# Splitting 768-column products into 384 and 384 columns, one half per PSUM bank, in place of 512 and 256

## The reference, cut to what matters

```python
for i in range(DEPTH):                     # DEPTH = 2
    h_lat = modulate(rmsnorm(x, g_mix_pre[i]), ...)
    h_ctx = modulate(rmsnorm(xc, g_mix_pre[i]), ...)
    if last:
        s_f, s_b = context_states(h_ctx, ...)      # k, v and decay columns of w_in alone
    else:
        y_ctx, s_f, s_b = token_mixer(h_ctx, *mix_w, s0, s0)
        xc = ffn_sublayer(xc + ..., ...)
    y_lat, _, _ = token_mixer(h_lat, *mix_w, s_f, s_b)   # p = h @ w_in; ... ; y @ w_out
    x = ffn_sublayer(x + ..., ...)                       # (silu(a) * u) @ w_ffn_out, a | u = h @ w_ffn_in
```

## Time and profile before

| what | value |
|---|---|
| time, median of 3 runs | 1666.36 us (1664.7 to 1668.96) |
| span of the profiled execution, first to last instruction | 1662.6 us |
| mean granted TensorE clock | 0.990 |
| PE busy | 1589.5 us, 96% |
| PEld busy | 1344.1 us |
| DVE, ACT, POOL busy | 729.6, 568.3, 587.4 us |

### The profile page before, as it was taken

How to read it: one execution, slowest core, us unless ns; L and a number is a source line. 1 busy time by engine, 2 the same in 40 slices (tenths; PEclk the granted TensorE clock), 3 DMA queues, 4 the chain that set the end, 5 groups by cost and what they waited for, 6 DMA issues and landing times.

```text
span 1662.6 us, 23266 instructions
## 1 busy us (share of the span) xinstructions
PE 1589.5 (96%) x9328; PEld 1344.1 (81%) x9328; DVE 729.6 (44%) x1206; ACT 568.3 (34%) x918; POOL 587.4 (35%) x309
## 2 busy tenths in 40 slices
PE   5999999999899999999999989999989999999997
PEld 2778877877689989998999767787877888888887
DVE  2500325845656515662366673045754321221137
ACT  4533213524634313441244254432523422232231
POOL 1522211334424524553255223222132444444441
PEclk9999999999999999999999999999999999999999
DMA  9444332154312212222122343531071222222221
GB/s 372 167 166 149 127 114 71 39 206 180 152 39 77 89 38 77 77 72 75 56 77 69 134 152 104 176 112 53 27 279 52 89 92 97 93 96 100 90 87 66
DMA packets 49166, 182.37 MB, mean 110 GB/s; under 512 B 5106, under 2 KB 10098, under 8 KB 42164
## 3 DMA queue, kind: packets, MB, share of 16 engines
q1 hardware_dynamic: 42930, 167.28, 28.5%
q10 hardware_dynamic: 6146, 13.83, 2.4%
HBM read 169.55 MB, written 11.53 MB: 109 GB/s over the span
## 4 chain that ended last, share of the span: by engine, by line
PE 85%; DVE 5%; ACT 3%; DMA 3%; POOL 1%; issue 1%; SPq 1%; DVEq 0%; ACTq 0%; POOLq 0%
PE A L981 58%; PE A L1227 8%; PE N L1227 4%; PE G L1227 4%; DMA raw<-stream 2%; PE N L1001 1%; PE G L1282 1%; DMA raw<-modw 1%; PE A L1123 1%; PE G L1089 1%; SPq L848 1%; PE G L1001 1%; PE N L1073 1%; PE G L1130 1%; PE A L1161 1%
## 5 line engine op out<-in xcount | busy, mean ns | idle before, releaser
L919 POOL TENSOR_TENSOR w_lo<-raw,w_hi 128x1024 fp32r<-128x1024 f32 (+2 forms) x163 | 379.9, 2333 | 709.9 <-ACT w_hi L1309 672.7
L981 PE MATMUL A<-h_hi,w_hi 128*128 128x512 f32 (+1 forms) x1264 | 415.8, 360 | 22.8 <-POOL h_lo L964 11.7
L981 PE MATMUL A<-h_hi,w_lo 128*128 128x512 f32 (+1 forms) x1264 | 406.7, 353 | 0.0
L981 PE MATMUL A<-h_lo,w_hi 128*128 128x512 f32 (+1 forms) x1264 | 405.9, 352 | 0.0
L1309 ACT ACTIVATE w_hi<-raw 128x1024 fp32r<-128x1024 f32 (+2 forms) x163 | 167.0, 1028 | 389.5 <-PE A L981 342.1
L981 PEld LDWEIGHTS A<-h_hi,w_hi 128*128 128x128 f32 x1264 | 223.2, 190 | 80.8 <-POOL h_lo L964 18.5
L981 PEld LDWEIGHTS A<-h_hi,w_lo 128*128 128x128 f32 x1264 | 223.9, 190 | 32.7
L981 PEld LDWEIGHTS A<-h_lo,w_hi 128*128 128x128 f32 x1264 | 223.4, 190 | 31.4 <-issue 0.5
L981 PE MATMUL A<-g_hi,w_hi 128*128 128x512 f32 (+1 forms) x480 | 147.8, 351 | 3.8 <-DVE g_lo L1790 2.0
L981 PE MATMUL A<-g_lo,w_hi 128*128 128x512 f32 (+1 forms) x480 | 146.8, 349 | 0.0
L981 PE MATMUL A<-g_hi,w_lo 128*128 128x512 f32 (+1 forms) x480 | 146.7, 349 | 0.0
(11 more groups left out here) (308 smaller groups left out, 2570.2 us busy)
## 6 DMA issues: line engine op xcount, KB each, us to landing
raw<-stream SPq DMA_DIRECT2D x150, 512.0 KB, 3.3
mraw<-modw SPq DMA_DIRECT2D x38, 1024.0 KB, 4.8
raw<-pairs SPq DMA_DIRECT2D x18, 512.0 KB, 4.7
raw<-modw SPq DMA_DIRECT2D x6, 1024.0 KB, 14.7
x<-x_keep ACTq DMA_DIRECT2D x4, 1536.0 KB, 14.3
raw<-stream SPq DMA_DIRECT2D x16, 384.0 KB, 3.0
mraw<-pairs SPq DMA_DIRECT2D x9, 512.0 KB, 3.4
x_keep<-x SPq DMA_DIRECT2D x4, 768.0 KB, 22.4
```

The source lines that it names most:

```text
L919: pool.tensor_tensor(lo, like_chunk(n, raw[:, n % RAW, 0:WIDTH[n]]), hi.bitcast(F32), ALU.subtract).then_inc(lo_done, 1)
L981: m = pe.matmul(dst[:, t0:t1], a, b[:, k, t0:t1], start=(first and p == 0), stop=(last and p == 2))
```

## The change

`in_banks` takes the place of `segments` in the products of 768 tokens: tokens 0 to 383 go to columns 0 to 383 of the accumulator's first bank, tokens 384 to 767 to columns 0 to 383 of its second bank (512 to 895 of the tile). `split_matmul` writes each range at the place `at` that comes with it. All the readers of these chunks use a two-part view of the accumulator (`out_banks`) and of their target (`by_bank`). Parts that are products of their own stay as they were (`own_part`).

```diff
+def in_banks(T):
+    return [(0, HALF, 0), (HALF, TOK, 512)] if T > SEQ else [(0, T, 0)]
...
+        def out_banks(j, T):
+            return A[j][:, :].rearrange("p (b t) -> p b t", b=2)[:, :, 0:HALF] if T > SEQ else A[j][:, 0:T]
+        def by_bank(t, T):
+            return t.rearrange("p (b t) -> p b t", b=2) if T > SEQ else t
...
-                    for t0, t1, _ in ranges:
-                        m = pe.matmul(dst[:, t0:t1], a, b[:, k, t0:t1], start=(first and p == 0), stop=(last and p == 2))
+                    for t0, t1, at in ranges:
+                        m = pe.matmul(dst[:, at:at + t1 - t0], a, b[:, k, t0:t1], start=(first and p == 0),
+                                      stop=(last and p == 2))
...
+            def own_part(e, s):
+                t0, t1, _ = parts(e)[s]
+                return [(t0, t1, t0)]
...
-                    project(A[PLAN.acc[e]], n0, segments(tokens(L, name)), H).then_inc(chunk_used, 1)
+                    project(A[PLAN.acc[e]], n0, in_banks(tokens(L, name)), H).then_inc(chunk_used, 1)
...
-                        project(A[j % 2], n0 + j, segments(tokens(L)), H).then_inc(chunk_used, 1)
+                        project(A[j % 2], n0 + j, in_banks(tokens(L)), H).then_inc(chunk_used, 1)
...
-                    ranges = segments(tokens(L)) if e[2] < 2 else [parts(e)[0]]
+                    ranges = in_banks(tokens(L)) if e[2] < 2 else own_part(e, 0)
...
+                    src = src[:, 0:T]
+                    if e[2] > 1:
+                        dst, src = by_bank(dst, T), out_banks(PLAN.acc[e], T)
...
-                        act.activation(sil[:, 0:TOK], A[0][:, 0:TOK], ACT.Silu).then_inc(free["A0"], 1)
+                        gate, a_out = (by_bank(sil[:, 0:TOK], TOK), out_banks(0, TOK)) if q else (sil[:, 0:TOK], A[0][:, 0:TOK])
+                        act.activation(gate, a_out, ACT.Silu).then_inc(free["A0"], 1)
...
-                        m = dve.tensor_tensor(cgz[:, j, 0:T], cgz[:, j, 0:T], A[PLAN.acc[e]][:, 0:T], ALU.mult)
+                        cu = by_bank(cgz[:, j, 0:T], T)
+                        m = dve.tensor_tensor(cu, cu, out_banks(PLAN.acc[e], T), ALU.mult)
...
-                        ym, src = y[:, j, :], A[j % 2][:, 0:TOK]
+                        ym, src = by_bank(y[:, j, :], TOK), out_banks(j % 2, TOK)
...
-                        dve.tensor_tensor(sil[:, 0:TOK], sil[:, 0:TOK], A[1][:, 0:TOK], ALU.mult).then_inc(free["A1"], 1)
+                        gate, u_out = (by_bank(sil[:, 0:TOK], TOK), out_banks(1, TOK)) if q else (sil[:, 0:TOK], A[1][:, 0:TOK])
+                        dve.tensor_tensor(gate, gate, u_out, ALU.mult).then_inc(free["A1"], 1)
```

More of the change, by code:

```diff
@@ L1039, in _ @@
                         pe.wait_ge(h_whole, len(LOW_V))
-                    m = project(dst, n, [parts(("nrm",) + pre)[s]], H, ready=lambda k: h_wait(pe, *pre, s, k))
+                    m = project(dst, n, own_part(("nrm",) + pre, s), H, ready=lambda k: h_wait(pe, *pre, s, k))
                     if s == len(parts(("nrm",) + pre)) - 1:
@@ L1048, in _ @@
                     dst = A[e[3] % 2][:, SEQ // 2:] if L else A[e[3] % 2]
-                    project(dst, n, [parts(e)[1]], src, K=K).then_inc(chunk_used, 1)
+                    project(dst, n, own_part(e, 1), src, K=K).then_inc(chunk_used, 1)
                 elif kind == "z":
@@ L1183, in _ @@
                             pe.wait_ge(free[f"A{j % 2}"], PLAN.acc[e][j % 2] + j // 2)
-                            project(A[j % 2], n0 + j, [parts(e)[0]], H, ready=ready, first=4).then_inc(half_done, 1)
+                            project(A[j % 2], n0 + j, own_part(e, 0), H, ready=ready, first=4).then_inc(half_done, 1)
                         continue
@@ L1189, in _ @@
                             pe.wait_ge(free[f"A{j % 2}"], 2 * i + (PLAN.acc[e][j % 2] + j // 2))
-                            project(A[j % 2], n0 + j, [parts(e)[0]], H, ready=ready, first=4).then_inc(chunk_used, 1)
+                            project(A[j % 2], n0 + j, own_part(e, 0), H, ready=ready, first=4).then_inc(chunk_used, 1)
                 elif kind == "ffn_in":
@@ L1430, in _ @@
                            "f": uF[:, j % 2, 0:T], "c": cgz[:, j % 2, 0:T], "b": bg[:, j % 2, 0:T], "r": r_s[:, j, 0:T]}[name]
+                    src = src[:, 0:T]
+                    if e[2] > 1:
+                        dst, src = by_bank(dst, T), out_banks(PLAN.acc[e], T)
                     if name == "r":
-                        m = act.activation(dst, src[:, 0:T], ACT.Silu)
+                        m = act.activation(dst, src, ACT.Silu)
                     else:
-                        m = act.activation(dst, src[:, 0:T], ACT.Copy, scale=DK ** -0.5 if name == "q" else 1.0)
+                        m = act.activation(dst, src, ACT.Copy, scale=DK ** -0.5 if name == "q" else 1.0)
                     m.then_inc(free[f"A{PLAN.acc[e]}"], 1)
```

## The result

The changed kernel takes 1657.88 us in the median of six runs (1656.16 to 1661.11), the kernel before 1667.38 us in six (1664.7 to 1668.96) beside them: ratio 0.9936, 95% interval 0.9917 to 0.9956. That is faster by 9.5 us, where 5.4 were forecast, and just under the range, which began at 1658.0. (The prediction knew three of the six runs before, with a median of 1666.36.) The span of the profiled execution is 1654.4 us, 8.2 less than before.

The account below looks back on a forecast made before the run. TensorE was taken to bound the kernel. Savings of 3.4 us on usual `h` chunks and 2.1 on `g`, less 0.1 on quick chunks, took the span from 1662.6 to 1657.2, plus 3.8 gives 1661.0 us; range 1658.0 to 1668.0.

Parts of the forecast that it names:

- What bounds the kernel: TensorE, busy 96% of the span; whatever a chunk gains or loses on it reaches the end of the kernel.
- The pair after: Two 384-column matmuls in `proj`, `ffn_in` and `ffn_out` cost 347.7 ns, as in `fast`, in place of 353.2.
- The sum of 5.4 us: Usual `h` chunks save 3.4 us, quick chunks lose 0.1, `g` chunks save 2.1: span 1662.6 to 1657.2.
- The `proj` stretch: Should shorten by some 2.0 us, 22 pairs of a chunk taking 7.65 us in place of 7.77.
- The four quick chunks: Four `proj` chunks already at 346.8 ns a pair, 96 pairs, go to 347.7: 0.1 us lost.
- The 6.5 ns: Excess per pair of 512 and 256 columns in 42 of 46 chunks, put at 6.3 ns over unmixed widths.
- The readers: ACT and DVE read 768 columns in two runs of 384 at no added cost; DVE takes 958 ns.
- The excess that stays: Rival: the 6.3 ns come from changing bank and columns with every matmul, so 1666.4 us; chance 0.17.
- the extra step on both halves: Rival: each 384-column matmul pays a step, a pair costs 360.7 ns, 1674 us, slower; chance 0.11.
- Only `h` gains: Rival: `g` in `ffn_out` stays dear, 351.4 to 361.6 ns a pair, so 1663 to 1665 us; chance 0.17.
- nothing outside should change its length: Stretches that the change doesn't touch keep their length, so the span falls by the sum alone, to 1657.2 us.
- the 3.8 us between span and median: The median of the runs lies 3.8 us above the profiled span; added to 1657.2 it gives 1661.0 us.

Follow-up runs that it names:

- experiment 2: All products of one half of a chunk before the other's: changed kernel (`half_by_half`) 1670.57 us, kernel before (`wide_then_narrow`) 1667.99 us.
- Experiments 5 and 6: Kernel before split into 448 and 320 columns (`split_448`), 1660.08 us in nine runs; changed kernel with buffers moved 32 bytes (`g_moved`), 1662.81 us in one.
- `split_448`: Kernel before with products split into 448 and 320 columns side by side, read in one run: 1660.08 us in nine runs, ratio 0.9947.
- experiment 4: Changed kernel with 13 more matmuls ahead of layer 0's last `proj` chunk, 1665.35 us; kernel before without 12 of that chunk's 48 matmuls, 1664.58 us.
- `g_moved`: Changed kernel with 32 unused bytes per partition ahead of buffers `y`, `g` and `x`: 1662.81 us in one run.
- `wide_then_narrow`: Kernel before with all 512-column matmuls of a chunk first, then all 256-column ones: 1667.99 us, ratio 0.9987.
- `after_late_look_3`: Traced execution of the changed kernel with 13 more matmuls ahead of the last `proj` chunk of layer 0: 1660.37 us at clock 0.989.
- `before_look_3`: Traced execution of the kernel before, unchanged: 1672.78 us at clock 0.984.
- `ffn_alone`: Changed kernel with equal halves only in `ffn_in` and `ffn_out`, `proj` kept at 512 and 256 columns: 1662.93 us, ratio 0.9971.
- `before_look_2`: Traced execution of the kernel before, unchanged: 1667.29 us at clock 0.990.
- `half_by_half`: Changed kernel with all products of a chunk's first half done before all of its second: 1670.57 us, ratio 1.0006.

## Why the prediction was right or wrong

**What bounds the kernel: right.** TensorE stays full in the windows (52.70 of 52.70 us and 67.00 of 67.00), and what the pairs gained reached the end of each stretch.

**The pair after: right in kind.** Forecast 347.7 ns; measured 346.7 on `h`, the lower bound that I named, and 349.3 on `g`. "22 pairs in 7.65 us" became 7.62, "a piece of 66.8 us" 67.07. The sum of 5.4 us, term by term: `h` 3.3 forecast, 2.30 + 0.94 + 0.53 = 3.8 measured; `g` 2.1 forecast, 1.5 measured. Together 5.3. The `proj` stretch was to shorten by 2.0 us and did by 2.3. The four quick chunks hardly changed, 8.52 us before and 8.52 to 8.55 after.

**The 6.5 ns.** The excess goes when 256 columns stand among themselves (120.0 ns, and 226.7 for 512, experiment 2) and when the narrow half has 320 columns (346.7 a pair, 5). It stays where 512 and 256 columns take turns (353.2). I suspected that the weight load for the wide matmul comes late behind the narrow one. No run isolated the load, and three things speak against it as the whole cause: the quick chunks of 512 and 256, the two slow ones of 448 and 320, and the place of the excess. In the trace before a usual chunk has its matmul of 512 columns start 84.38 - 84.26 = 0.12 us after that of 256, no later than in a stream of 256 alone, and the next one of 256 starts 84.62 - 84.38 = 0.24 us after that. Over the chunk's pairs the means are 117 and 236 ns, in the quick chunk from 72.01 us on 117 and 230. If the load for the wide matmul came late behind the narrow one, the first distance should have grown; it is the second that did, so far as recorded starts can tell. What costs the 6.5 ns stays open.

**Cost and width.** Among their own kind matmuls of `h` start 120.0, 173.3 and 226.7 ns apart at 256, 384 and 512 columns. These lie on one line: (226.7 - 120.0) / 256 = 0.417 ns a column, by which 384 columns would take 120.0 + 128 x 0.417 = 173.4. By that line, an estimate of mine, any split of 768 columns into two costs 2 x 120.0 + 256 x 0.417 = 346.7 ns. It holds for 384 and 384, and for 448 and 320 in 17 of 19 chunks; of the three splits tried 512 and 256 in turn costs 6.5 ns a pair more. The matmuls of 130 columns, 111.5 ns apart, lie above the line as well, which would give them an estimated 120.0 - 126 x 0.417 = 67.5.

**The readers: right**, 957 ns for 958, and `split_448` with its plain reads ends at the same time.

**The rivals.** The excess that stays and the extra step on both halves fell with the first trace. *Only `h` gains* is half true in kind: `g` gained 3.9 ns a pair and not 6.5. Experiments 5 and 6 show that this is not its being `g`: at 448 and 320 columns, or with the buffers 32 bytes on, it costs 346.7. Nor was the 351.4 that this rival took from layer 1 the cost of `g` unmixed in layer 0, which is 346.8 (experiment 2).

**What failed** is the step from the sum to a time: "nothing outside should change its length". The span was to fall by the sum alone, 5.4 us, to 1657.2, and fell by 8.2, to 1654.4. The sum itself held (5.3), and so did the 3.8 us between span and median (3.5 after). What was put at nothing is 3.2 us between 909 and 982 us, where the trace before has two stretches at half clock (from 910.2 and 954.6 us, 3.4 us each) and the trace after none. The range took over the same mistake: its lower end, "6.6 us, and 1.8 us of spread between runs", has no room for a clock that differs. I counted TensorE at a granted clock of 1.00 throughout, though the earlier trace rows showed 1.00 only for the stretches that I had asked for, and the mean of the whole was 0.990. That missing hundredth is 34 us at half clock in the trace before, up to 17 us of time by my estimate (34 / 2), and it is no constant.

The gain over many runs then has three parts. The rates give 5.3 us. The 13.7 us stretch comes, by the one such run that was traced, with the runs above 1671 us, 46 of 110, which lift the mean of the kernel before from 1666.0 us (the 64 others) to 1669.0: 3.0 us, and the earlier arrival takes this away, as experiment 4 shows from both sides. The rest: 1666.0 less 1659.3 (mean of 15 runs after) is 6.7 us, 1.4 more than the rates; the medians of the same runs, 1665.5 and 1660.0, differ by 5.5. This remainder would be the shorter stretches. Those at 910 and 955 us stand in all four traces of the kernel before and in neither of the changed one's two. Of the other twelve traces ten have the later, `g_moved` among them, whose instructions are the changed kernel's; `wide_then_narrow` has the earlier too, and `after_late_look_3` the earlier alone. Others, such as that at 1213 us after and that at 1248 us in two traces of before, make up for some of it. Whether the change does away with these two on average, and how, stays open.

The first measurement's six runs of before had none above 1669 us, and still lay 9.5 us over the changed kernel's. The long stretch has no part in that. The rates and the two stretches explain 5.3 + 3.2 = 8.5 us of it, if the profiled executions are typical of the twelve runs, which isn't shown; by the larger sets, 5.5 to 6.7 were to be expected without the long stretch. So between 1 and 4 us of the 9.5 may be chance in which six runs were met.

Also open: what decides, at a given arrival, whether the stretch comes. `before_look_3` reached a place just ahead of it (`osq`, L1169) at 330.32 us and had it; `ffn_alone` reached it at 330.41 and had not. No trace that reached it before 329.98 had it.

## What to carry to other kernels

When one product of 768 columns needs two matmuls with a weight load each, try splits whose shorter part is well over 256 columns: here equal halves and 448 and 320 did about equally well in the kernel's time (ratios 0.9945 and 0.9947), 512 and 256 in turn didn't, and changing the bank with each matmul cost nothing (8.53 us a chunk with it and without). Making all of one half first gains the same in the chunks, but it asks for the last input block twice as early, and here the waits (3.2 us, twice) took back what it had gained. For changes well under 1%, read the granted clock over the whole span of several traces before and set the sum against that; this change of 5 us by its rates measured 9.5 in the first six runs of each kernel.

## What the runs showed of the hardware that was not expected

- A stretch of small matmuls ran at a granted clock of 0.50 in one execution (`before_look_3`, 13.7 us from 332.5 us on) and at 1.00 in another (`before_look_2`) of the same program: 5.9 us of time. An arrival 2.25 us later made it appear in a trace of the changed kernel, and one 2.1 us earlier left no run that clearly has it.
- Work after a wait of TensorE is where the halving was seen: 3.2 us of waiting in `half_by_half` came with 6.8 us at half clock in one block and 3.4 in the next, 2.0 us in `wide_then_narrow` with 3.4, where the kernels without the wait had none.
- Streams of matmuls of `h` with a weight load each take 120.0, 173.3 and 226.7 ns a matmul at 256, 384 and 512 columns, on one line of 0.417 ns a column. Those of `g` take 6.5 ns less at 256 columns (113.5), 1.4 more at 384 (174.7) and 6.6 more at 512 (233.3). 512 in turn with 256 costs 6.5 ns a pair more in 42 of 46 chunks.
- Moving buffers by 32 bytes changed a 384-column matmul of `g` from 174.7 to 173.3 ns, and made the `fast` ones dearer by about 0.7 ns on average (96 of them 16.76 us for 16.69), some of `h` among them, which hadn't moved.
